# A small VectorE copy moved ahead of sixteen matrix builds, and two gate steps moved from inside the attention stage to behind it, in a fused two-block model kernel on one core

## The reference

```python
q_l, k_l, v_l = mla_qkv(qlat_l, kvlat_l, krope_l, ...)
y_mla_l = attend(q_l, concat([k_c, k_l]), concat([v_c, v_l]))       # 8 heads, 256 queries, 512 keys
x_c = silu(dwconv(x_m))
q = blockdiag(x_c, w_qblk); k = blockdiag(x_c, w_kblk); v = blockdiag(x_m, w_vblk)   # 4x4 blocks
hl = mlstm_bidir(...)                                              # the "cells"
y_ml = sigmoid(z_l) * (rms(hl) * ml_norm + ml_skip * x_c)
out = (sigmoid(g_mla) * y_mla_l + sigmoid(g_ml) * y_ml) @ w_out
x = x + g1 * out
x = x + g2 * ec_moe(modulate(rmsnorm(x)), w_router, w_e_gate, w_e_up, w_e_down)      # 16 experts
```

## Time and profile before

| | |
|---|---|
| time, median of 3 executions | 2101.92 us (2101.23 to 2105.65) |
| the profiled execution | 2101.23 us |
| its span, first to last instruction | 2099.4 us |
| TensorE, matmuls | busy 1878.0 us, 89% |
| VectorE | busy 755.3 us, 36% |
| ScalarE | busy 532.1 us, 25% |
| mean granted TensorE clock | 0.957 of full speed |
| DMA | 414.14 MB, mean 197 GB/s |

### The profile page before, as it was taken

The page is one execution under the profiler, slowest core; times in us unless marked ns, Lnnn a source line. Parts: engine busy times, 40 slices in busy tenths (PEclk is TensorE's granted clock), DMA queues, the critical chain, the costliest instruction groups (busy, mean ns, idle before and its releaser), DMA issues.

```text
span 2099.4 us, 26157 instructions
## 1 busy us (share of the span) xinstructions
PE 1878.0 (89%) x11342; PEld 1435.6 (68%) x11342; DVE 755.3 (36%) x1242; ACT 532.1 (25%) x804; POOL 0.2 (0%) x4
## 2 busy tenths in 40 slices
PE   6999999999998999999999999999999886656555
PEld 5789877899997898776899999545788521111101
DVE  2442332556534532332566675522444300000001
ACT  2201122254341101122254454333542210000001
POOL 0000000000000000000000000000000000000000
PEclk9999999999999999999999999999999988787877
DMA  6222342555432221444655431120115999999997
GB/s 258 101 87 74 129 158 96 200 201 186 168 148 80 89 113 61 177 184 178 244 209 188 154 136 66 61 80 5 41 76 209 425 427 428 427 427 427 428 428 317
DMA packets 30643, 414.14 MB, mean 197 GB/s; under 512 B 3392, under 2 KB 3648, under 8 KB 4288
## 3 DMA queue, kind: packets, MB, share of 16 engines
q1 hardware_dynamic: 29808, 408.69, 48.7%
q10 hardware_dynamic: 720, 3.78, 0.4%
HBM read 411.41 MB, written 1.05 MB: 196 GB/s over the span
## 4 chain that ended last, share of the span: by engine, by line
PE 72%; DMA 19%; DVE 5%; ACT 2%; issue 1%; another core or an unknown queue 0%; DVEq 0%; ACTq 0%
PE ps L220 55%; PE ps L755 7%; DMA low<-in_w_e_up_dram 5%; DMA ring<-in_w_e_gate_dram 5%; DMA low<-in_w_e_down_dram 4%; PE ps L1147 3%; PE ps L1177 3%; DMA high<-in_w_e_up_dram 2%; DMA low<-in_w_e_gate_dram 2%; DVE high L179 2%; PE ps L1514 2%; ACT high L214 1%; DVE high L189 1%; PE ps L1403 1%; DMA ring<-in_w_in_dram 1%
## 5 line engine op out<-in xcount | busy, mean ns | idle before, releaser
L220 PE MATMUL ps<-high,ring 128*128 128x256 f32 (+1 forms) x2016 | 479.7, 389 | 9.4 <-DMA ring<-in_w_in_dram 4.4
L220 PE MATMUL ps<-rarena 128*128 128x256 f32 (+1 forms) x3648 | 453.4, 287 | 0.0
L220 PEld LDWEIGHTS ps<-rarena 128*128 128x128 f32 x3648 | 445.4, 191 | 6.3
L220 PEld LDWEIGHTS ps<-high,ring 128*128 128x128 f32 x2016 | 375.4, 192 | 80.0 <-issue 21.0
L214 ACT ACTIVATE high<-ps 128x512 f32<-128x512 f32 (+2 forms) x210 | 103.3, 492 | 687.0 <-PE ps L220 244.9
L214 ACT ACTIVATE rarena<-ring 128x2048 fp32r<-128x2048 f32 x76 | 140.0, 1842 | 257.4 <-PE ps L220 195.7
L179 DVE TENSOR_TENSOR rarena<-ring,rarena 128x2048 fp32r<-128x2048 f32 x76 | 167.3, 2201 | 97.5 <-ACT rarena L214 96.3
L179 DVE TENSOR_TENSOR high<-high,ps 128x512 f32<-128x512 f32 x52 | 35.7, 687 | 304.8 <-PE ps L1514 247.0
L755 PE MATMUL ps<-high 128*128 128x128 f32 (+6 forms) x1024 | 127.1, 295 | 11.7 <-DVE high L179 10.7
L755 PEld LDWEIGHTS ps<-high 128*128 128x128 f32 (+2 forms) x1024 | 110.6, 189 | 32.5 <-issue 14.2
L1514 PE MATMUL ps<-high,low 128*32 128x512 f32 x592 | 89.4, 732 | 47.0 <-DMA high<-in_w_e_up_dram 30.3
(11 more groups left out here) (160 smaller groups left out, 1557.1 us busy)
## 6 DMA issues: line engine op xcount, KB each, us to landing
ring<-in_w_in_dram SPq DMA_DIRECT2D x36, 2048.0 KB, 7.5
ring<-in_w_ffn_up_dram SPq DMA_DIRECT2D x22, 2048.0 KB, 7.7
high<-in_w_e_up_dram SPq DMA_DIRECT2D x20, 2048.0 KB, 50.3
high<-in_w_e_gate_dram SPq DMA_DIRECT2D x17, 2048.0 KB, 47.7
high<-in_w_e_down_dram SPq DMA_DIRECT2D x17, 2048.0 KB, 49.6
ring<-in_w_mod_dram SPq DMA_DIRECT2D x12, 2048.0 KB, 9.0
ring<-in_w_e_down_dram SPq DMA_DIRECT2D x10, 2048.0 KB, 50.3
ring<-in_w_ffn_down_dram SPq DMA_DIRECT2D x8, 2048.0 KB, 7.3
```

What stands on the lines that cost most here:

```text
L220: ins = self.e.matmul(out, l, r, start=first and i == 0, stop=end and i == n - 1)
```

## The change

Three edits. VectorE's copy of `crow` moves from behind all 24 builds to behind the first eight, together with its wait for TensorE's `crow` sum. The two extra fill steps after mixer step 47 are taken out. The stage after attention has four fill steps ahead of `crow` in place of two. The four engines' programs all read the two constants; the fill steps before the cells are 14 in both. With the change attention holds fill steps 0 to 9 (step 9, the end of gm0, after n = 50) and stage 3 holds steps 10 to 13 (gm1 and gm2).

```diff
                     V.stt(T.BD[:, z, i, :].rearrange("p (n k) -> p n k", k=4),
                           pc(nm, 4 * i, 4).unsqueeze(1).to_broadcast([128, 32, 4]), 1.0 if z else 1.0 / 16,
                           c("bd").rearrange("p (n k) -> p n k", k=4), mul, mul).then_inc(*V(f"bd{z}{i}"))
-            V.wait_ge("crow.ps")
-            V.cp(crow, ps("crow.ps")[:, 0:16]).then_inc(*V("crow"))
+                if z == 0:
+                    V.wait_ge("crow.ps")
+                    V.cp(crow, ps("crow.ps")[:, 0:16]).then_inc(*V("crow"))
             mix([none(QK_STEPS)], fill, [1], False)
...
-AT_PLAN[47] += 2
-QK_STEPS = 2
+QK_STEPS = 4
```

## The result

The changed kernel takes 2114.84 us (median of 5, 2113.96 to 2116.21) against 2103.76 us (median of 5, 2101.23 to 2105.65) for the kernel before: ratio 1.0054, interval 1.0043 to 1.0064. Forecast were 2109.4 us and 2105.4 to 2112.4. The loss is 11.1 us where the sum gave 8.2, and the baseline of the sum, one execution of 2101.23 us, is 2.5 us under the median of before. The profiled execution of after took 2112.22 us (span 2110.4), so the two profiles are 11.0 us apart, as the medians are.

What follows compares the result with a forecast made beforehand. The expert-load stream, started by TensorE's last gate unit, was taken to set the end; +5.9 us of order and +2.3 us of clock on 2101.23 us gave 2109.4 us, 8-in-10 range 2105.4 to 2112.4.

Steps and rivals of the forecast that it cites:

- the sum: Whole kernel: +5.9 us of order to tq7's start plus 2.3 us of clock, +8.2 us on 2101.23 us.
- What bounds the kernel: Experts' stage: ends when its 96 loads have streamed at 427 GB/s; the first load waits for TensorE's last gate unit.
- moves the last gate unit, the first load and the end, one for one: Between attention and the cells: each microsecond TensorE loses or gains shifts the first expert load and kernel end equally.
- Two fill steps out of attention: Attention's last transposes: 3.45 us of work removed, but VectorE's divisions limit the gain to 0.83 us.
- The moved copy: VectorE's building stage: waits almost 6 us for crow after eight builds, so the other 16 end at 1497.0.
- the pairs: VectorE behind the builds: two gate pairs, 0.86 us each, precede its tq1 copy; tq7 starts at 1499.2.
- ScalarE behind the pair: ScalarE's queue: gm2's tanh waits for gm0's pair, delaying tq0's copy; TensorE idles 4.7 us, tq6 at 1498.7.
- The clock: TensorE behind gaps of 4.3 and 4.7 us: half clock costs 0.7 and 1.6 us, together 2.3, between 0 and 4.6.
- The baseline: Starting time: the profiled execution's 2101.23 us, with the shown median 2101.92, 0.7 us higher, left inside the range.
- The wait is hidden: Rival at tq6: VectorE finishes before TensorE needs the bank; +1.1 us, 2102.3 us, no measurable change; chance 0.08.
- absorbed: Rival before the expert stream: it still starts at 1609.6 and the time stays 2101.2 us; chance 0.05.
- More is lost: Rival: both gaps cost 2.3 us or more and late ScalarE delays the cells; 2112 us and up; chance 0.07.

Runs made afterwards that it cites:

- with the clock held: Changed kernel plus unread matmuls in TensorE's two new gaps (8 before the last transposes, 10 before tq6): 2112.59 us against 2115.09 for the changed kernel.
- after + 1.3 us: Changed kernel plus three unread 128x256 matmuls behind the cells, delaying the first expert load 1.3 us; profiled twice; ratio to before 1.0054.
- after with the end kept up: Changed kernel plus five unread 128x256 matmuls behind each of five down loads in the last expert group: 2115.81 us, ratio to before 1.0037.
- the third profile of before: Kernel before the change, nothing edited, profiled a third time: 30.59 us from flip matmul to v1, 489.7 us from first expert load to end.
- the same delayed kernel: Kernel before the change plus five unread 128x256 matmuls behind the cells (2.15 us), profiled twice; ratio to before 1.0016.

## Why the prediction was wrong, point by point

- *What bounds the kernel.* Right up to the first load. Every loss or gain of the stretch came out there in full (108.85 us from v1 to the load in all). The step that failed is the next one, "moves the last gate unit, the first load and the end, one for one": from the first load to the end the changed kernel took 2.1 us more in both profiles. The DMA rate is 427 GB/s as forecast; what isn't one for one is TensorE's clock in the router, where 0.6 us goes, and over the last expert's matmuls, where 1.4 goes. Keeping TensorE at work there took the 1.4 us away. That the 0.6 us is the clock in the router was only seen in the windows (0.54 in both profiles of after, 0.70 to 0.77 in three of before), not tried.
- *Two fill steps out of attention.* Forecast 0.83 us won, measured 0.89 at full clock (7.32 against 8.21 us from flip matmul to head 6) and 0.57 in the changed kernel.
- *The moved copy, the pairs, ScalarE behind the pair.* Right, each within 0.3 us: `crow` read at 1491.76 (forecast 1491.55), builds over at 1497.15 (1497.0), tq6 at 1499.01 (1498.7), gap 4.60 (4.7). Order together: +5.80 us with the clock held, forecast +5.9.
- *The clock.* Right that both gaps drop it, mis-sized: 3.15 us where I took 2.3. The late gap cost 2.8, not 1.6, and more than my upper end of 2.3 for one gap, because the clock fell 1 us before the gap was over and stayed low for another 5.8. The early one cost 0.3, not 0.7. This split isn't fixed: three more executions whose order up to the cells is that of the changed kernel (after + 1.3 us twice, after with the end kept up) had 1.3 to 1.6 us behind the early gap and 1.7 behind the late one, and came to nearly the same sum, 39.4 to 39.65 us from flip to v1. The Trainium skill ("TensorE: Matmul & The Clock Gate", section "HAM oscillation — how this bites in real kernels") says that a TensorE that sits idle long enough ahead of a burst starts it at the slow clock. Both gaps here agree with it, with 0.50 behind each; the 17 us at 0.50 in the third profile of before came without such a gap, behind a stretch in which TensorE was busy 15.3 of 17 us.
- *The baseline.* I set the sum on 2101.23 us and left the 0.7 us to the shown median inside the range. The median of five is 2103.76, those of the later groups 2103.9 to 2107.7. That is 2.5 us of the 5.4 by which the time was missed; the rest is 0.85 of clock in the stretch, 2.05 behind the first load, and the order's 0.1 the other way, 2.8 together, with 0.1 left over. Either miss alone would have left the time inside the range: 2103.76 + 8.2 is 2112.0, and 2101.23 + 11.1 is 2112.3, just inside. That the sum's baseline was a low execution was bad luck, which a second profile would have shown.
- *The rivals.* "The wait is hidden" and "absorbed" didn't happen. "More is lost" was the right one in size (11.1 us), by a mechanism that I hadn't named: not a late ScalarE in the cells, but the low clock in a stage that the change doesn't touch.

What stays open: whether the 2 us in the experts' part belong to the change as a rule. Both profiles of after had them and none of the three of before, and the medians (11.1 us apart) fit that. But the change with three gate buffers had 490.0 us, and the same delayed kernel had 491.4 and 489.9. So the 2 us aren't a cost of the work itself; they go with where the low clock falls in the stage, and what decides that is not shown. It takes many profiles of each to tell how often it happens.

## What to carry to other kernels

A wait placed in the middle of an in-order engine's row of work delays all that stands behind it, even where the waiting operation itself is 0.17 us long: look for who needs the operations behind it, on every engine. Edits that look like one idea can feed each other (2.4 and 4.2 us alone, 9 together), so time them apart and together. And set a sum on the distance between two marks inside the trace, not on the time of one execution: the distance from flip to v1 repeated within 0.1 us in every kernel profiled twice, while 26 executions of the kernel before spread from 2099.8 to 2115.7.

## What was not expected of the hardware

- After a TensorE gap of 4.6 us the granted clock was 0.50 for another 5.8 us of solid matmul work in two executions, so half the price of the gap again (2.8 us) came behind it. In three others the same gap cost 1.7 us.
- In three of 17 executions the clock was 0.50 from 1457 to 1474 us, where TensorE was busy all the time, with the same work at 1.00 in the others. It costs 8.1 us.
- The same untouched experts' stage took from 489.7 to 493.5 us while the DMA engines were full (share 1.01 from 1660 to 2080 us in before and after), by which matmuls met the low clock. Useless matmuls between those of the last loads held the clock: each group of 16 behind them took 1.92 us in three kernels, and up to 3.64 us without them.
